# Four DMA turns of a feed-forward moved from SyncE's queue to ScalarE's

## The chip, the cores and the metric

The kernel runs on 1 core of one Trainium2 chip. The metric is the device time of one execution in microseconds; the kernel before has a median of 1064.58 us in 3 runs (1063.89 to 1068.48). TensorE, VectorE (DVE), ScalarE (ACT), GpSimd (POOL) and SyncE (SP) each work through a queue of their own and meet by semaphores.

## The reference

Two layers over x of 256 rows by 1024, all in float32. Each layer is: a half-step SwiGLU feed-forward, a token mixer, and a second half-step feed-forward. The change touches the feed-forwards alone:

```python
def _swiglu(h, w_gate, w_up, w_down):
    return (jax.nn.silu(h @ w_gate) * (h @ w_up)) @ w_down

x = x + 0.5 * _swiglu(_rms_norm(x, ffn1_norm[l]), ffn1_w_gate[l], ffn1_w_up[l], ffn1_w_down[l])
```

with D_MODEL 1024 and D_FF 2816. The mixer (a convolution of width 31, latent attention with 8 heads, gates and an output projection) stands between the two feed-forwards of a layer.

## The kernel before

**Products in three parts.** Every float32 product is made of three float32r products on TensorE: high by high, low by high and high by low (`products`, lines 602 to 606). So each weight unit of 128 x 2048 is loaded by SP into one of 3 raw buffers, rounded by ScalarE into `whi` (`split`, line 1044), and its rest is written by VectorE into `wlo` (`split`, line 1390). `whi` and `wlo` are rings of 6 units. SP may load a unit once VectorE has finished the rest of the unit three before it (`place`, line 360 issues).

**A feed-forward.** There are four, named (l, f) here: layer l, half f. D_FF is cut into NCH = 11 chunks of 256 columns. Chunk c has two units of gate and up weights and one of down weights, so the units of a feed-forward are: 0 and 1 for gate_up(0), then 2, 3 for gate_up(1), 4 for down(0), 5, 6 for gate_up(2), 7 for down(1), and so on; 32 is down(10), and in a first half 33 and 34 are the mixer's first two (w_in). TensorE does gate_up(c) for row tiles t = 0 and 1 (24 matmuls each), then down(c - 1) for both (12 each). Between gate_up(c) and down(c) the chunk's value has to be transposed:

- ScalarE `silu(c, t)` (line 1101) and VectorE `mul(c, t)` (line 1465) make the gated value of a row tile in `gu`.
- ScalarE `split_planes(c, t)` (line 1110) rearranges it as 16-bit words into `planes`, which lies in tile `qkT`; it counts up `planes_ready`.
- A DMA transposes `planes` into `turned`, also in `qkT`: this is the turn (`plane_turn`, line 385, `dma_start_transpose`). It waits for both planes and for `joined` of the turn before, so one turn is in flight at a time.
- VectorE `join(c)` (line 1478) puts the words together again in `vtok`, ScalarE `round_joined(c)` (line 1118) rounds to `gThi`, VectorE `rest_joined(c)` (line 1395) writes `gTlo`, and TensorE's down(c) waits for that.

The last chunk, c = 10, is transposed by TensorE instead (`turn`, line 716; `round_gu`, line 1126; `rest_gu`, line 1395); this `rest_gu` stands in VectorE's queue behind the split of unit 33 in a first half.

**Orders written out by hand.** SP's order in a feed-forward (lines 391 to 408) is gate_up(c) units, then the turn of chunk c - 2, then down(c - 1), for c from 1 to 10. The turn of chunk 9 (NCH - 2) stands outside: after a first half between the two halves of the first w_in block (line 431), after the second half of layer 0 in the next layer's first loads (line 400), and at the very end (line 451). ScalarE's order in chunk 0 is `first` (line 1129): split 2, silu(0,0), squares, split 3, planes(0,0), silu(0,1), split 4, planes(0,1). In chunks 1 to 9 it is `pair` (line 1140): round_joined of the chunk before, split, silu, split, planes, silu, split, planes. VectorE's has join(c - 1), rest_joined(c - 1), then split, mul, split, mul, split (lines 1487 ff.); in chunk 0 split 4 is its last item ahead of join(0). At the end ScalarE splits unit 32, then does round_joined(9), silu(10,0) and, in a first half, split 33.

Of the kernel before, what the change touches and what calls it, by code (L numbers as in the profile page):

```python
# [27 lines left out]
DEPTH = 2  # L28
# [86 lines left out]
def trunk(nc, a):  # L115
    with ExitStack() as ctx:
# [190 lines left out]
        def per_turn(l, f, c):  # L307
            return (l * 2 + f) * (NCH - 1) + c + 1
# [45 lines left out]
        @block.sync  # L354
        def _(sp):
            def place(l, u, u0, pairs):

                sp.wait_ge(wlo_ready, l * U_LAYER + u + 1)
                for dst, src in pairs:
                    sp.dma_start(dst, src).then_inc(raw_landed[slot(u0, RAW)], 16)  # L360

            def gate_up(l, f, c, c0, h):
                u0 = unit_gu(f, c0, h)
                dst = raw[:, slot(u0, RAW), 0:2048].rearrange("p (k g n) -> p k g n", k=4, g=2)
                rows = slice(4 * h * P, 4 * (h + 1) * P)
                cols = bass.ds(c * FC, FC)
                place(l, unit_gu(f, c, h), u0, [
                    (dst[:, :, g, :], w[l, rows, cols].rearrange("(k p) n -> p k n", p=P))
                    for g, w in enumerate((wg[f], wu[f]))])

            def down(l, f, c, c0):
                u0 = unit_down(f, c0)
                dst = raw[:, slot(u0, RAW), 0:2048].rearrange("p (k n) -> p k n", k=2)
                place(l, unit_down(f, c), u0, [
                    (dst[:, k, :], wd[f][l, bass.ds(c * FC + k * P, P), :]) for k in range(2)])

            def load_gain(l):

                sp.dma_start(gain[:, :], norms[1][bass.ds(l, 1), :].to_broadcast([P, D])).then_inc(gain_landed, 16)

            def plane_turn(l, f, c):

                sp.wait_ge(planes_ready, per_turn(l, f, c) * TT)
                sp.wait_ge(joined, per_turn(l, f, c))
                sp.dma_start_transpose(turned[:, :, :], planes.rearrange("p b k t f -> p (b k t f)")
                                       ).then_inc(turned_landed, 16)

            def ffn(l, f):
                def first():
                    if l == 0 and f == 0:  # L390
                        first_unit(sp, 0, 0)
                        second_tile(sp, 0)
                        first_unit(sp, 1, 0)
                        for t in range(TT):
                            sp.dma_start(posi[:, t:t + 1], a["positions"][0, t * P:(t + 1) * P].unsqueeze(1)
                                         ).then_inc(small_landed, 16)
                    else:
                        gate_up(l, f, 0, 0, 0)
                        if f == 0:
                            plane_turn(l - 1, 1, NCH - 2)  # L400
                        gate_up(l, f, 0, 0, 1)

                first()
                for c in range(1, NCH):
                    gate_up(l, f, c, c, 0)
                    gate_up(l, f, c, c, 1)
                    if c > 1:
                        plane_turn(l, f, c - 2)
                    down(l, f, c - 1, c - 1)
                down(l, f, NCH - 1, NCH - 1)  # L410

            def block_of(l, u, w, r0, k, c0, n):

                dst = raw[:, slot(u, RAW), 0:k * n].rearrange("p (k n) -> p k n", k=k)
                src = w[l, r0:r0 + k * P, c0:c0 + n].rearrange("(k p) n -> p k n", p=P)
                h = k // 2
                place(l, u, u, [(dst[:, h:k], src[:, h:k]), (dst[:, 0:h], src[:, 0:h])])

            sp.dma_start(x[:, 0, 0:512], a["x"][0, 0:P, 0:512]).then_inc(x_first, 16)

            for l in range(DEPTH):
                ffn(l, 0)
                load_gain(l)

                sp.wait_ge(vec_used, l + 1)
                sp.dma_start(vec[:, :], a["vec"][l]).then_inc(vec_landed, 16)
                for n, w in enumerate((a["q_norm"], a["k_norm"])):
                    sp.dma_start(qkg[:, n, :], w[bass.ds(l, 1), NOPE:QK].to_broadcast([P, ROPE])).then_inc(vec_landed, 16)
                for h in range(2):
                    if h == 1:  # L430
                        plane_turn(l, 0, NCH - 2)
                    block_of(l, UM + M_PR + h, a["w_in"], 4 * h * P, 4, O1, PR)
                def conv_units(base, j):
                    for g in range(2):
                        block_of(l, UM + base + g, a["w_in"], 0, KD, g * C + j * 256, 256)

                conv_units(M_C01, 0)
                block_of(l, UM + M_UQ, a["w_uq"], 0, 2, 0, H * QK)
                block_of(l, UM + M_UKV, a["w_ukv"], 0, 2, 0, H * (NOPE + VD))
                conv_units(M_C23, 1)  # L440
                for g in range(4):
                    for h in range(2):
                        block_of(l, UM + M_G + 2 * g + h, a["w_in"], 4 * h * P, 4, O4 + g * C, C)
                for h in range(2):
                    block_of(l, UM + M_MLA + h, a["w_mla_out"], 2 * h * P, 2, 0, D)
                for h in range(2):
                    block_of(l, UM + M_CO + h, a["w_conv_out"], 2 * h * P, 2, 0, D)
                for h in range(4):
                    block_of(l, UM + M_WO + h, a["w_out"], 2 * h * P, 2, 0, D)
                ffn(l, 1)  # L450
            plane_turn(DEPTH - 1, 1, NCH - 2)

            sp.wait_ge(x_new, 6 * DEPTH + 1)
            sp.dma_start(a["out"][0, 0:P, :], x[:, 0, :]).then_inc(stored, 16)
            for h in range(2):
                sp.wait_ge(last_new, h + 1)
                sp.dma_start(a["out"][0, P:SEQ, h * 512:(h + 1) * 512], x[:, 1, h * 512:(h + 1) * 512]).then_inc(stored, 16)
            sp.wait_ge(gain_landed, 16 * DEPTH)
            sp.wait_ge(stored, 16 * 3)
# [578 lines left out]
        def _(act):  # L1038
            def split(l, u0, turns=0):

                n = (l * (U_LAYER // RAW) + turns + (u0 // RAW + 1)) * 32
                act.wait_ge(raw_landed[slot(u0, RAW)], n)
                act.wait_ge(unit_free, l * U_LAYER + turns * RAW + (u0 + 1))
                nc.scalar.activation(whi[:, slot(u0, RING), 0:USED[u0]], raw[:, slot(u0, RAW), 0:USED[u0]],  # L1044
                                     ACT.Copy).then_inc(whi_ready, 1)
# [47 lines left out]
            def ffn(l, f):  # L1093
                def silu(c, t):
                    if t == 0:
                        act.wait_ge(gu_done, l * (2 * NCH) + c + (NCH * f + 1))
                    else:
                        unit_released(act, l, unit_gu(f, c, 1))
                    if isinstance(c, int) and c == 0:
                        act.wait_ge(rs_ready, per_norm(l, 2 * f, t))  # L1100
                    nc.scalar.activation(sgate[:, t, :], bank[:, 4 + t, 0:FC], ACT.Silu,  # L1101
                                         scale=rs[:, t:t + 1]).then_inc(silu_ready, 1)

                def split_planes(c, t):
# [4 lines left out]
                    words = gu[:, t, :].bitcast(U16).rearrange("p (k f b) -> p b k f", k=2, b=2)  # L1109
                    nc.scalar.activation(planes[:, :, :, t, :], words, ACT.Copy).then_inc(planes_ready, 1)  # L1110

                def round_joined(c, c0):

                    act.wait_ge(joined, per_turn(l, f, c) + 1)
                    if not (isinstance(c, int) and c == 0):

                        unit_released(act, l, c * 3 + (UB[f] - 2))
                    nc.scalar.activation(gThi[:, (c0 % 2) * 2:(c0 % 2) * 2 + 2, :], g_turned.rearrange("p (k n) -> p k n", k=2),  # L1118
                                         ACT.Copy).then_inc(ghi, 2)
# [10 lines left out]
                def first():  # L1130
                    split(l, UB[f] + 2)
                    silu(0, 0)
                    norm_squares(l, 2 * f, 1)
                    split(l, UB[f] + 3)
                    split_planes(0, 0)
                    silu(0, 1)
                    split(l, UB[f] + 4)
                    split_planes(0, 1)

                def pair(c, c0, i=0):  # L1140
                    u = UB[f] + 2 + 3 * c0
# [10 lines left out]
                with act.Fori(0, (NCH - 3) // 2) as i:  # L1152
                    pair(i * 2 + 1, 1, i * 2)
                    pair(i * 2 + 2, 2, i * 2)
                pair(NCH - 2, NCH - 2)
                c = NCH - 1
                if f == 0:
                    split(l, UB[f] + 2 + 3 * c)
# [686 lines left out]
```

## Time and profile before

| | |
|---|---|
| median of 3 runs | 1064.58 us (1063.89 to 1068.48) |
| profiled execution | 1062.78 us, span 1060.9 us |
| PE busy | 1048.6 us |
| DVE busy | 673.2 us |
| ACT busy | 560.1 us |
| POOL busy | 229.5 us |
| granted TensorE clock | 1.000 of full |
| bytes moved | 205.06 MB, 193 GB/s on average |
| DMA issues of w_down units, half a unit each | 88, 512.0 KB, median 5.4 us to landing |

A busy time is the sum over an engine's instructions; TensorE's matmuls overlap, so neighbours start closer together than each lasts. In the timelines a row begins with its start in us from the span's start and its duration; the bracket at its end is the idle time of the engine before it and what ended it. TensorE's first down product stands at 35.15 us in (0,0), 375.03 in (0,1), 556.87 in (1,0) and 899.09 in (1,1).

### The profile page before, as it was taken

What the parts mean: (1) busy time and instruction counts of PE and PEld (TensorE: products, weight loads), DVE (VectorE), ACT (ScalarE), POOL (GpSimd) and SP (SyncE); (2) the same over time, 40 slices, a digit from 0 to 9 for tenths busy, and PEclk for the clock granted to TensorE, in tenths of its full rate; (3) what the DMA queues carried; (4) which work ended last, traced back from release to release, by engine and by line L of the source; (5) the groups of instructions that cost most, each with busy time, mean ns of one, the idle gap of its engine ahead of it and who ended that gap; (6) DMA issues with size and microseconds to landing.
All of it is one profiled execution on the core that took longest, in us unless ns stands there. A gap on an engine that the chain in (4) does not pass through costs nothing. (4 is left out here: it accounts for less than half of the span.)

```text
span 1060.9 us, 13912 instructions
## 1 busy us (share of the span) xinstructions
PE 1048.6 (99%) x5100; PEld 878.8 (83%) x5100; DVE 673.2 (63%) x899; ACT 560.1 (53%) x732; POOL 229.5 (22%) x258
## 2 busy tenths in 40 slices
PE   8999999999999999999999999999999999999998
PEld 5888887998888888888888888879988887888887
DVE  6556556599976465565656546556999665564563
ACT  6445445575762554454455535536767535454461
POOL 1840000049850000000048000002589300000000
PEclk9999999999999999999999999999999999999999
DMA  8776786365645367767656686674366345867761
GB/s 277 220 230 202 211 242 225 127 219 169 208 149 179 95 203 218 225 200 219 217 159 204 186 249 204 206 247 157 132 209 232 105 159 129 220 203 220 225 203 48
DMA packets 176701, 205.06 MB, mean 193 GB/s; under 512 B 49264, under 2 KB 147856, under 8 KB 176656
## 3 DMA queue, kind: packets, MB, share of 16 engines
q1 hardware_dynamic: 174064, 200.78, 61.3%
q10 hardware_dynamic: 2592, 3.69, 1.2%
q8 instruction: 27, 0.44, 0.2%
q14 instruction: 18, 0.15, 0.0%
HBM read 192.90 MB, written 1.05 MB: 183 GB/s over the span
## 5 line engine op out<-in xcount | busy, mean ns | idle before, releaser
L1390 DVE TENSOR_TENSOR wlo<-raw,whi 128x2048 fp32r<-128x2048 f32 x154 | 351.4, 2286 | 69.1 <-ACT whi L1044 69.0
L604 PE MATMUL bank<-whi,hThi 128*128 128x512 f32 (+1 forms) x976 | 379.2, 388 | 0.3 <-DVE wlo L1390 0.3
L606 PE MATMUL bank<-whi,hTlo 128*128 128x512 f32 (+1 forms) x976 | 373.7, 383 | 0.0
L605 PE MATMUL bank<-wlo,hThi 128*128 128x512 f32 (+1 forms) x976 | 373.6, 383 | 0.0
L1044 ACT ACTIVATE whi<-raw 128x2048 fp32r<-128x2048 f32 x178 | 338.7, 1908 | 16.2 <-DMA raw<-in_ffn_w_up 7.9
L604 PEld LDWEIGHTS bank<-whi,hThi 128*128 128x128 f32 x976 | 183.4, 188 | 36.0 <-DVE wlo L1390 0.7
L606 PEld LDWEIGHTS bank<-whi,hTlo 128*128 128x128 f32 x976 | 183.2, 188 | 35.8
L605 PEld LDWEIGHTS bank<-wlo,hThi 128*128 128x128 f32 x976 | 183.5, 188 | 34.2
L1118 ACT ACTIVATE gThi<-vtok 128x512 fp32r<-128x512 f32 x40 | 25.3, 632 | 277.1 <-DVE vtok L1478 237.8
L604 PE MATMUL bank<-whi,gThi 128*128 128x512 f32 (+1 forms) x416 | 162.7, 391 | 2.7 <-DVE gTlo L1395 2.7
L605 PE MATMUL bank<-wlo,gThi 128*128 128x512 f32 (+1 forms) x416 | 161.2, 387 | 0.0
L606 PE MATMUL bank<-whi,gTlo 128*128 128x512 f32 (+1 forms) x416 | 161.2, 387 | 0.0
L472 POOL TENSOR_TENSOR small<-small,expo 128x1 f32<-128x1 f32 (+3 forms) x20 | 21.7, 1087 | 602.6 <-DVE small L1399 562.5
L1478 DVE COPY vtok<-qkT 128x1024 uint16<-128x1024 uint16 x40 | 30.2, 755 | 166.6 <-DMA qkT<-qkT 166.4
L586 POOL TENSOR_TENSOR wlo<-raw,whi 128x2048 fp32r<-128x2048 f32 x24 | 110.2, 4604 | 19.1 <-ACT whi L1044 18.8
L1557 DVE SCALAR_TENSOR_TENSOR bank<-cu,vec,bank 128x256 f32<-128x256 f32 x240 | 97.3, 484 | 0.1
L604 PEld LDWEIGHTS bank<-whi,gThi 128*128 128x128 f32 x416 | 78.1, 188 | 19.7 <-DVE gTlo L1395 4.3
L606 PEld LDWEIGHTS bank<-whi,gTlo 128*128 128x128 f32 x416 | 78.1, 188 | 16.1
L605 PEld LDWEIGHTS bank<-wlo,gThi 128*128 128x128 f32 x416 | 78.2, 188 | 15.3
L1110 ACT ACTIVATE qkT<-gates 128x512 uint16<-128x512 uint16 x80 | 50.0, 625 | 23.9 <-DVE gates L1465 23.9
L1101 ACT ACTIVATE gates<-bank,small 128x256 f32<-128x256 f32 x88 | 40.5, 460 | 19.1 <-PE bank L606 17.8
L1395 DVE TENSOR_TENSOR gTlo<-vtok,gThi 128x512 fp32r<-128x512 f32 x40 | 27.7, 692 | 35.5 <-ACT gThi L1118 35.5
(163 smaller groups left out, 805.8 us busy)
## 6 DMA issues: line engine op xcount, KB each, us to landing
raw<-in_ffn_w_down SPq DMA_DIRECT2D x88, 512.0 KB, 5.4
raw<-in_ffn_w_gate SPq DMA_DIRECT2D x86, 512.0 KB, 4.2
raw<-in_ffn_w_up SPq DMA_DIRECT2D x86, 512.0 KB, 5.3
raw<-in_w_in SPq DMA_DIRECT2D x48, 512.0 KB, 4.9
raw<-in_w_out SPq DMA_DIRECT2D x16, 512.0 KB, 4.4
raw<-in_w_in SPq DMA_DIRECT2D x8, 544.0 KB, 7.6
raw<-in_w_mla_out SPq DMA_DIRECT2D x8, 512.0 KB, 3.9
raw<-in_w_conv_out SPq DMA_DIRECT2D x8, 512.0 KB, 4.8
```

The source lines that it names most:

```text
L586: nc.gpsimd.tensor_tensor(wlo[:, slot(u, RING), 0:n], raw[:, slot(u, RAW), 0:n], whi[:, slot(u, RING), 0:n].bitcast(F32), ALU.subtract).th ...
L604: nc.tensor.matmul(out, lh, rh, start=start, stop=False, skip_group_check=skip)
L605: nc.tensor.matmul(out, lh, rl, start=False, stop=False, skip_group_check=skip)
L606: return nc.tensor.matmul(out, ll, rh, start=False, stop=stop, skip_group_check=skip)
L1044: nc.scalar.activation(whi[:, slot(u0, RING), 0:USED[u0]], raw[:, slot(u0, RAW), 0:USED[u0]], ACT.Copy).then_inc(whi_ready, 1)
L1101: nc.scalar.activation(sgate[:, t, :], bank[:, 4 + t, 0:FC], ACT.Silu, scale=rs[:, t:t + 1]).then_inc(silu_ready, 1)
L1110: nc.scalar.activation(planes[:, :, :, t, :], words, ACT.Copy).then_inc(planes_ready, 1)
L1118: nc.scalar.activation(gThi[:, (c0 % 2) * 2:(c0 % 2) * 2 + 2, :], g_turned.rearrange("p (k n) -> p k n", k=2), ACT.Copy).then_inc(ghi, 2)
L1390: nc.vector.tensor_tensor(wlo[:, slot(u0, RING), 0:n], raw[:, slot(u0, RAW), 0:n], whi[:, slot(u0, RING), 0:n].bitcast(F32), ALU.subtract) ...
L1395: return nc.vector.tensor_tensor(out, in_, hi.bitcast(F32), ALU.subtract)
L1478: nc.vector.tensor_copy(g_turned.bitcast(U16).rearrange("p (n b) -> p b n", b=2), turned.rearrange("p (b j) r -> p b (j r)", b=2)).then_in ...
L1557: ins = nc.vector.scalar_tensor_tensor(out=o, in0=i, scalar=w, in1=o, op0=ALU.mult, op1=ALU.add)
```

## The change

The turns of chunk 0 and of chunk 9 of every feed-forward are issued by ScalarE; those of chunks 1 to 8 stay with SP. ScalarE issues the turn of chunk 9 right behind planes(9,1), ahead of the split of unit 32. In chunk 0 planes(0,1) moves ahead of split 4, and the turn stands between the two. The waits of a turn are the same ones.

```diff
@@ SP
                     else:
                         gate_up(l, f, 0, 0, 0)
-                        if f == 0:
-                            plane_turn(l - 1, 1, NCH - 2)
                         gate_up(l, f, 0, 0, 1)
...
-                    if c > 1:
+                    if c > 2:
                         plane_turn(l, f, c - 2)
                     down(l, f, c - 1, c - 1)
...
                 for h in range(2):
-                    if h == 1:
-                        plane_turn(l, 0, NCH - 2)
                     block_of(l, UM + M_PR + h, a["w_in"], 4 * h * P, 4, O1, PR)
...
                 ffn(l, 1)
-            plane_turn(DEPTH - 1, 1, NCH - 2)
@@ ScalarE
+                def plane_turn(c):
+
+
+                    act.wait_ge(planes_ready, per_turn(l, f, c) * TT)
+                    act.wait_ge(joined, per_turn(l, f, c))
+                    act.dma_start_transpose(turned[:, :, :], planes.rearrange("p b k t f -> p (b k t f)")
+                                            ).then_inc(turned_landed, 16)
...
                     split_planes(0, 0)
                     silu(0, 1)
+                    split_planes(0, 1)
+                    plane_turn(0)
                     split(l, UB[f] + 4)
-                    split_planes(0, 1)
...
                 pair(NCH - 2, NCH - 2)
+                plane_turn(NCH - 2)
                 c = NCH - 1
```

## Rows read from the trace of the kernel before

**Rows 1.** DMA issues, whole span: count, KB each, median us to landing
```profile
raw<-in_w_in SPq DMA_DIRECT2D x8, 544.0 KB, 7.6
...
bias<-in_gate_bias ACTq DMA_DIRECT2D x8, 256.0 KB, 4.3
```

**Rows 2.** Waits of TensorE's weight loads: us in total, times, longest us
```profile
PEld bank L604 <- DVE gTlo L1395: 4.3, 4, 1.2
```

**Rows 3.** TensorE's timeline at its stalls: start us, us, what, [idle before <-releaser]
```profile
34.04 0.39 PE L605 MATMUL bank<-wlo,hThi 128*128 128x512 f32 x1
34.27 0.39 PE L606 MATMUL bank<-whi,hTlo 128*128 128x512 f32 x1
35.15 0.50 PE L604 MATMUL bank<-whi,gThi 128*128 128x512 f32 x1 [0.49 <-DVE gTlo L1395]
...
183.50 0.50 PE L604 MATMUL bank<-whi,gThi 128*128 128x512 f32 x1 [0.68 <-DVE gTlo L1395]
...
702.78 0.44 PE L716 MATMUL bank<-ident,gates 128*128 128x128 f32 x2 [1.59 <-DVE gates L1465]
...
706.65 0.50 PE L604 MATMUL bank<-whi,gThi 128*128 128x512 f32 x1 [0.68 <-DVE gTlo L1395]
...
899.09 0.50 PE L604 MATMUL bank<-whi,gThi 128*128 128x512 f32 x1 [0.80 <-DVE gTlo L1395]
```

**Rows 4.** ScalarE's timeline, (1,1), first chunk
```profile
887.45 0.47 ACT L1101 ACTIVATE gates<-bank,small 128x256 f32<-128x256 f32 x1 [0.92 <-PE bank L606]
887.82 1.91 ACT L1044 ACTIVATE whi<-raw 128x2048 fp32r<-128x2048 f32 x1
889.63 0.61 ACT L1110 ACTIVATE qkT<-gates 128x512 uint16<-128x512 uint16 x1
```

**Rows 5.** VectorE's timeline, (1,1), first chunk
```profile
888.26 0.48 DVE L1465 SCALAR_TENSOR_TENSOR gates<-bank,small,gates 128x256 f32<-128x256 f32 x1
889.76 2.29 DVE L1390 TENSOR_TENSOR wlo<-raw,whi 128x2048 fp32r<-128x2048 f32 x1 [1.02 <-ACT whi L1044]
896.69 0.75 DVE L1478 COPY vtok<-qkT 128x1024 uint16<-128x1024 uint16 x1 [4.63 <-DMA qkT<-qkT]
```

**Rows 6.** SP's timeline, (1,1), first chunk
```profile
890.27 1.25 SPq L385 DMA_TRANSPOSE qkT<-qkT  x1
892.08 0.86 SPq L360 DMA_DIRECT2D raw<-in_ffn_w_down  x2
```

**Rows 7.** VectorE's and SP's timelines, (0,0), first chunk
```profile
26.06 0.48 DVE L1465 SCALAR_TENSOR_TENSOR gates<-bank,small,gates 128x256 f32<-128x256 f32 x1
...
32.73 0.76 DVE L1478 COPY vtok<-qkT 128x1024 uint16<-128x1024 uint16 x1 [3.90 <-DMA qkT<-qkT]
...
27.23 1.92 SPq L385 DMA_TRANSPOSE qkT<-qkT  x1
```

**Rows 8.** ScalarE's, VectorE's and SP's timelines, (1,0), its end
```profile
689.99 0.61 ACT L1110 ACTIVATE qkT<-gates 128x512 uint16<-128x512 uint16 x1
...
701.80 2.01 ACT L1044 ACTIVATE whi<-raw 128x2176 fp32r<-128x2176 f32 x1
...
700.07 0.75 DVE L1478 COPY vtok<-qkT 128x1024 uint16<-128x1024 uint16 x1 [4.30 <-DMA qkT<-qkT]
...
706.18 0.42 DVE L1395 TENSOR_TENSOR gTlo<-bank,gThi 128x256 fp32r<-128x256 f32 x1
...
690.84 3.40 SPq L385 DMA_TRANSPOSE qkT<-qkT  x1
```

**Rows 9.** VectorE's and SP's timelines, (0,0), its end
```profile
176.91 0.75 DVE L1478 COPY vtok<-qkT 128x1024 uint16<-128x1024 uint16 x1 [3.94 <-DMA qkT<-qkT]
...
168.86 2.23 SPq L385 DMA_TRANSPOSE qkT<-qkT  x1
```

**Rows 10.** Tile qkT: all turns, ns min/median/max of the issue; us to landing
```profile
L385 SPq DMA_TRANSPOSE qkT<-qkT x40: 1232/2048/3403, 27.2 to 1032.9; - x40
...
DMA to landing us min/median/max: 3.0/6.2/9.2
```


## The prediction

> **What bounds the kernel now.** I read the page first, then the waits of TensorE, then the timelines of all queues around each place where TensorE waited. The page (the table above) has TensorE busy for 1048.6 us of 1060.9: only what lets TensorE wait costs time. Its 512-column matmuls start 0.23 us apart while each lasts 0.39 [rows 3], so a wait loses the idle time in the brackets plus 0.16 us, and the first matmul behind it lasts 0.50 instead of 0.39: another 0.11. Among the waits of the weight loads the largest with a releaser is gTlo L1395, the feed-forward's transposed operand: 4.3 us in 4 times [rows 2]. Naming a feed-forward (layer, half), the stalls that count are:
> - (0,0), first chunk's down product: 0.49 + 0.16 + 0.11 = 0.76 us.
> - (0,0), end: 0.68 + 0.27 = 0.95 us, at 183.50.
> - (1,0), end: 1.59 + 0.16 = 1.75 us before the transposes at 702.78, and 0.68 + 0.27 = 0.95 at 706.65.
> - (1,1), first chunk: 0.80 + 0.27 = 1.07 us, at 899.09.
> Together 5.5 us, 0.5% of the time [rows 3]. The middle two feed-forwards' first chunks do not stall, nor do the ends of (0,1) and (1,1). That 5.5 us is all the change can reach.
>
> **Why they stall.** First chunk of (1,1): ScalarE does silu(0,1) at 887.45, split 4 (887.82, 1.91 us), planes(0,1) at 889.63 (0.61 us) [rows 4]; SP issues the turn at 890.27 [rows 6]; VectorE joins at 896.69 [rows 5]: 6.42 us for a turn whose landing times over the kernel are 3.0/6.2/9.2 us [rows 10]. TensorE gets its operand 2.40 us behind the join's start (899.09 - 896.69) [rows 3, 5]. End of (1,0): turn issued at 690.84, join at 700.07, 9.23 us later [rows 8]. SP's order (lines 431 and 432) puts a w_in block's loads (median 7.6 us to landing [rows 1]) right ahead of it in the same queue. I read this as a turn that lands when what stands ahead of it in SP's queue has landed. The last turn, with nothing left to load beside it, lands in the 3.0 us of [rows 10].
>
> **First chunk, four times.** Moved ahead of split 4: planes(0,1) and the turn. Put behind them: split 4. Removed: nothing. Planes(0,1) now waits for mul(0,1) on VectorE, which split 4 used to cover: in (1,1) mul ends at 888.26 + 0.48 = 888.74 [rows 5], planes run 888.77 to 889.38, and the turn goes at 889.43, 0.84 us earlier than before. The turn holds ScalarE's queue. No row shows a turn issued from ScalarE; SP's take 1.23 to 3.40 us, median 2.05 [rows 10]. The long ones stand where loads fill SP's queue (3.40 at 690.84 [rows 8]); the one at 890.27 takes 1.25 and the next issue comes 1.81 behind it [rows 6]. ScalarE's queue is empty here, so I take D = 1.81 us, and keep 1.25 and 3.40 as ends. Split 4 then starts at 889.43 + D, takes 1.91, VectorE's half 2.29 [rows 4, 5], and that half stands ahead of the join in VectorE's order: the join can't start before 889.43 + D + 4.23 = 895.47. Its operand is there 2.40 later, 897.87; TensorE is ready at 898.13 (899.09 - 0.96). The stall of 1.07 goes if the turn lands by 895.73, that is within 6.3 us. Gain 1.07.
> The slack is thus 898.13 - 897.87 + 1.81 - D = 2.07 - D. The first chunks of (0,1) and (1,0) have the same order around them and TensorE at the same pace, so the same slack holds: 0.26 us are left at D = 1.81, and they stay without a stall.
> (0,0) differs. There mul(0,1) ran late, from 26.06 to 26.54, and the turn went at 27.23 [rows 7]. Planes can't run earlier, so the turn isn't issued any earlier, while split 4, which filled the wait for mul, is now pushed to 27.23 + D: join not before 27.23 + D + 4.23 = 33.27, where it was 32.73 [rows 7]. Here the edit costs 0.54 us (nothing at D = 1.25, 2.1 at 3.40).
> Sum of the first chunks: 1.07 - 0.54 = +0.5 us gained.
> SP, freed of the turn, still can't load down(1) at once: the raw buffer is released by split 4's VectorE half, in (1,1) now at 895.5 against 892.08 before [rows 6]. Its split comes behind the join (0.75), round_joined, two other splits (1.91 each), two silu and planes, over 6 us, and such a load lands in 5.4 us (the table's median): hidden, by about a microsecond at the least, and not late for TensorE, which wants it a chunk later.
>
> **Last but one chunk, four times.** The turn goes right behind planes(9,1) from ScalarE, ahead of one split. In (1,0): planes end at 689.99 + 0.61 = 690.60, turn at 690.65, nearly as before (690.84); the gain is the other queue. What landing on its own queue? Lower end 3.0 [rows 10], upper end the 9.2 of before; small loads from ScalarE's queue land in 4.3 us (median, 256 KB) [rows 1], the nearest row, also beside SP's loads; I take 4.5. The split behind the turn starts at 690.65 + D = 692.46, its VectorE half ends at 692.46 + 1.91 + 0.03 + 2.29 = 696.7, and the join follows there instead of at 700.07 [rows 8]. Then silu(10,0) waits for TensorE alone, and TensorE's wait of 1.75 goes. The second stall hangs on what follows: from the start of split 33 at 701.80 to the end of rest_gu at 706.18 + 0.42 pass 4.80 us [rows 8]. TensorE, with both waits gone (706.65 - 0.84 - 1.75), wants that at 704.06. Silu(10,0) can start once gate_up(10,0) is done, 12 matmuls of 0.23 before 701.03, at 698.3; split 33 (0.35 behind it, as silu and split follow each other in [rows 4]) at 698.65, if w_in is there: issued up to 1 us ahead of 690.84 with a median of 7.6, and the turn now shares the engines with it, so 697.5 to 700. That gives rest_gu at 703.5 to 704.8, a rest of 0 to 0.8; I count half of 0.95 as gone. Gain 1.75 + 0.5 = 2.2 us, between 0 (landing of 9.2) and 2.7.
> (0,0), end: turn at 168.86, join at 176.91 [rows 9]; with 4.5 us to land the join comes at about 175 (behind the delayed split), w_in (ahead of 168.86 by up to 1 us, median 7.6) has landed when silu(10,0) is through, and I take the 0.95 as gone, between 0 and 1.1. Gain 0.9.
> (0,1) and (1,1), ends: ScalarE stood idle for long before round_joined, so D is hidden; the join comes up to 1.7 us later and is still ahead of TensorE. 0, and -0.5 at the longest D.
> SP's w_in loads behind the old turn go up to 1.9 us sooner; hidden.
>
> **Sum.** 0.5 + 2.2 + 0.9 = 3.6 us off the profiled execution's 1062.78 us (span 1060.9). That execution lies 1.8 us under the median of 1064.58; I carry the difference over: 1064.58 - 3.6 = 1061.0 us. With both ends: best 1.07 + 0 + 2.7 + 1.1 = 4.9 gained, worst below.
>
> **A rule that speaks against it.** The rows show turns landing right behind what SP's queue holds [rows 8, 10], and 4.3 us for ScalarE's loads [rows 1]. The Trainium skill (DMA: Bandwidth & Descriptors, "Issuing engines are not separate DMA queues") says that transfers from several issuing engines end up on the same 16 DMA engines and interleave, so that another issuer saves only the issue time. The same page ("Queues, rings and completion order") has each DMA engine take turns between rings, packet by packet, which would let the short turn overtake. No row shows a turn beside a full other queue. By the first alone the gains at the ends vanish (sum 0.4 us), which is the first rival; by the second they come as forecast (3.6 us).
>
> **Rivals.**
> - First: no overtaking. The turn on ScalarE's queue lands as late as before, since the same engines move the same bytes: 9.2 us behind its issue in (1,0). Then both ends give 0. The first chunks give +0.9 in (1,1) (issued 0.84 earlier) and -0.54 in (0,0): 0.4 us, 1064.2. For it: the loads ahead of the turn keep the same engines busy. Against: ScalarE's 256 KB loads at 4.3 us [rows 1].
> - Second: slower. ScalarE is held as SP at its worst, D = 3.40. By the slack 2.07 - D each first chunk stalls 1.33 + 0.11: -2.1 in (0,0), -1.4 in (0,1) and (1,0) each, -0.4 in (1,1), sum -5.3; ends +2.1. Net 3.2 slower: 1067.8. It decides at D of about 2.8, where the gains at the ends are used up. For it: the SP median of 2.05 is near the slack. Against: SP's long ones have a full queue ahead, ScalarE's has none.
> - Third: all four stalls go, w_in lands in time and ScalarE is held for 1.25 us: 4.9 us, and more where the turns of unprofiled executions land later than in this profile (the runs reach 1068.48): 1059.0.
> - Fourth: no effect, as TensorE's lost time returns at the mixer, whose inputs could be late by themselves. Nothing in the slices of the page has TensorE below 9 tenths behind the start, so I see no such place. 1064.5.
>
> **How the numbers follow.** Forecast 0.50, first rival 0.16, second 0.08, third 0.21, fourth 0.05. What a measurement of this kernel can tell is about 0.5%, 5.3 us. The forecast, the first and the fourth lie within it; the third is at its edge, half of it beyond (0.10), with 0.04 from the forecast where turns of the timed runs landed later than the profile's; the second passes it only beyond D = 3.9: 0.03 with what I can't name. So faster 0.14, same 0.83, slower 0.03. The range, 1058.5 to 1065.5, holds the forecast, the first, the fourth and most of the third, and leaves out the far half of the second and what lies beyond the third.
>
> **What would show it.** DMA_TRANSPOSE on ACT's queue eight times, 1.2 to 1.8 us each (second rival: above 2.5); turns at the ends of (0,0) and (1,0) landing in 3.5 to 5.5 us (first rival: 8 to 9); no idle TensorE before the transposes at the end of (1,0); (1,1)'s first chunk without a stall; (0,0)'s first stall grown from 0.49 idle to about 1.0; SP's down(1) load 3 to 4 us later. If the first chunks of (0,1) and (1,0) stall, the slack was misread.

## The result, and the profile after

The changed kernel takes 1074.03 us in the median of 20 runs (1066.12 to 1077.84), the one before 1063.96 us in 20 runs beside it (1060.25 to 1068.48). The ratio is 1.009, with a 95% interval of 1.0074 to 1.0105: slower by 0.9%. (A ratio in this document is not exactly the quotient of the two medians.) I had forecast 1061.0 us and a range up to 1065.5.

The profiled execution (1067.3 us, span 1065.2) is among the quick ones of these 20; a second profile of the same kernel, below, shows a common one.

**What went as forecast.** Tile qkT of the changed kernel, the turns by issuing queue (ns min/median/max of the issue), then us to landing; answers to [rows 10]:

```profile
L385 SPq DMA_TRANSPOSE qkT<-qkT x32: 1238/1574/3047, 42.6 to 1020.8; - x32
...
L1111 ACTq DMA_TRANSPOSE qkT<-qkT x8: 1249/1273/3951, 27.2 to 1037.2; - x8
...
DMA to landing us min/median/max: 3.1/5.8/14.3
```

Eight turns come from ScalarE, with a median of 1.27 us for the issue, but one is issued in 3.95 us, and one lands after 14.3 us where the longest was 9.2. TensorE's timeline at the first down products of (0,0), (0,1) and (1,1); answers to [rows 3]:

```profile
35.49 0.50 PE L598 MATMUL bank<-whi,gThi 128*128 128x512 f32 x1 [0.86 <-DVE gTlo L1399]
...
374.13 0.39 PE L598 MATMUL bank<-whi,gThi 128*128 128x512 f32 x1
...
903.43 0.50 PE L598 MATMUL bank<-whi,gThi 128*128 128x512 f32 x1 [0.41 <-DVE gTlo L1399]
```

(0,0)'s wait grew from 0.49 to 0.86 idle, (1,1)'s fell from 0.80 to 0.41. The two nearly cancel. ScalarE's timeline in (1,1) shows how long the issue holds it:

```profile
894.16 1.27 ACTq L1111 DMA_TRANSPOSE qkT<-qkT  x1
895.54 1.92 ACT L1038 ACTIVATE whi<-raw 128x2048 fp32r<-128x2048 f32 x1 [1.41 <-issue]
```

Split 4 starts 1.38 us behind the issue, where I took D = 1.81.

The end of (0,0) has no stall in this profile, as forecast, but its turn took 6.5 us to land: more than the 3.5 to 5.5 that I had named as the sign.

**Where the time went.** TensorE's timeline at the end of (1,0); answers to 702.78 and 706.65 of [rows 3]:

```profile
699.93 0.39 PE L600 MATMUL bank<-whi,hTlo 128*128 128x512 f32 x1
706.57 0.69 PE L710 MATMUL bank<-ident,gates 128*128 128x128 f32 x2 [6.25 <-DVE gates L1469]
706.91 0.78 PE L598 MATMUL bank<-whi,gThi 128*128 128x512 f32 x1
...
708.76 0.63 PE L599 MATMUL bank<-wlo,gThi 128*128 128x512 f32 x1
...
710.85 0.39 PE L598 MATMUL bank<-whi,gThi 128*128 128x512 f32 x1
```

The wait before the transposes is 6.25 us idle instead of 1.59. Behind it, nine matmuls take from 706.91 to 710.85, 3.94 us instead of 9 x 0.23 = 2.07. That is the granted clock (PEclk, as a share of full speed), in TensorE's columns of the windows of the changed kernel (us, busy and count of each engine, then PEclk, DMA share, GB/s):

```profile
695.00:706.00 11.00, 5.32 (x24) 4.08 (x22) 3.61 (x3) 1.86 (x4) 0.00 (x0) 0.91 1.09 244
706.00:711.00 5.00, 4.43 (x12) 3.62 (x13) 3.89 (x5) 3.77 (x3) 0.00 (x0) 0.52 0.15 54
711.00:716.00 5.00, 5.00 (x24) 4.14 (x23) 2.93 (x2) 0.29 (x1) 0.00 (x0) 1.00 0.97 319
```

0.52 is the 1.2 GHz level for nearly all of that stretch. It had already fallen while TensorE stood idle (0.91 over the stretch that ends at 706), and was back at 2.4 GHz from 711. Before, behind its wait of 1.59 us idle, the same columns read:

```profile
700.00:706.00 6.00, 4.38 (x20) 3.00 (x18) 4.00 (x4) 5.08 (x5) 0.00 (x0) 1.00 0.93 326
```

Against 2.7 us lost there before, this end now loses 6.4 of wait (706.57 - 699.93 - 0.23) and about 1.9 of clock (3.94 - 2.07): 5.6 us more. The old second stall (0.95) is absent, as the slow matmuls give its input time. The end of (0,0) gained: the first down product of (0,0) starts 0.34 us later than before, that of (0,1) 0.90 us earlier (374.13 against 375.03), so 1.2 us were won between them. The two first chunks cancel, and the sum is 5.6 - 1.2 = 4.4 slower (the span says 4.3).

ScalarE's, VectorE's and SP's timelines at that end; answers to [rows 8]:

```profile
689.58 3.95 ACTq L1111 DMA_TRANSPOSE qkT<-qkT  x1
693.64 1.92 ACT L1038 ACTIVATE whi<-raw 128x2048 fp32r<-128x2048 f32 x1 [4.08 <-issue]
...
695.59 2.29 DVE L1394 TENSOR_TENSOR wlo<-raw,whi 128x2048 fp32r<-128x2048 f32 x1 [4.22 <-ACT whi L1038]
703.87 0.74 DVE L1482 COPY vtok<-qkT 128x1024 uint16<-128x1024 uint16 x1 [5.99 <-DMA qkT<-qkT]
...
688.23 0.45 SPq L426 DMA_DIRECT2D qkg<-in_k_norm  x1
688.72 10.16 SPq L360 DMA_DIRECT2D raw<-in_w_in  x6
```

The turn goes out 1.3 us earlier than before (689.58), 0.9 of it because TensorE itself is 0.9 us ahead here, and is joined 3.8 us later (703.87 against 700.07). SP, which used to issue the turn between the halves of w_in, now issues w_in straight through: the second half starts at 691.39, before at 694.29 behind the turn (SP's timelines, the changed kernel and the one before).

```profile
691.39 2.59 SPq L360 DMA_DIRECT2D raw<-in_w_in  x2
```

```profile
694.29 12.92 SPq L360 DMA_DIRECT2D raw<-in_w_in  x6
```

The DMA packets of 694 to 697 us, then 697 to 700 us, in the changed kernel (q1 is SP's queue, q10 ScalarE's; packets, MB, share):

```profile
q1 hardware_dynamic: 317, 0.60, 114.1%
q10 hardware_dynamic: 107, 0.03, 17.7%
...
q1 hardware_dynamic: 267, 0.54, 54.6%
q10 hardware_dynamic: 541, 0.14, 39.5%
```

Both queues share the engines from the turn's first packets on. Before, all of them stood in q1, the turn ahead of w_in's second half.

### The profile page after: what moved, and what is told of

Same layout as the page of the kernel before. It is cut to its first block and busy times, and to the rows that moved or that the text cites. A ratio compares the mean times of both kernels' runs of the same rounds, so it can differ in the third digit from the quotient of the medians.

```text
span 1065.2 us, 13912 instructions
## 1 busy us (share of the span) xinstructions
PE 1050.9 (99%) x5100; PEld 880.8 (83%) x5100; DVE 674.0 (63%) x899; ACT 562.3 (53%) x732; POOL 229.8 (22%) x258
```

## The experiments

Each names the kernel that it starts from; times are medians, with the kernel before beside them on the same chip, and ratios are to it. Where one time stands alone, the one before is that of the runs just above. A stall's "idle" is the time in its bracket.

**Which half of the change.** First chunk only (from before; SP's turns from c > 2, ScalarE's order as changed, turn of chunk 9 left with SP):

```diff
                     silu(0, 1)
+                    split_planes(0, 1)
+                    plane_turn(0)
                     split(l, UB[f] + 4)
-                    split_planes(0, 1)
```

> Chunk 0's half of the change alone: planes ahead of split 4 and the turn from ScalarE; the turns of chunk 9 stay with SP. Theory (the loss sits at the ends of the first halves, where the turn on ScalarE's own queue has to share the DMA engines with w_in loads that SP issues behind it): within 1.5 us of the kernel before, the wait before the first down product 0.8 to 1.2 us in (0,0) and under 0.7 in (1,1). Rival (ScalarE held by the issue, first chunks pay): 5 us or more slower.

Measured: 1061.71 against 1061.8 us, ratio 1.0006 (0.9992 to 1.002), with waits of 0.89 idle at (0,0)'s first chunk and 0.40 at (1,1)'s. This half is free. Last but one chunk only (from before; SP's turns of chunk 9 are taken out, which the cut leaves out):

```diff
                 pair(NCH - 2, NCH - 2)
+                plane_turn(NCH - 2)
```

> Chunk 9's half of the change alone. Theory: it holds the whole loss, 5 to 12 us slower than the kernel before, with a turn at the end of (1,0) that takes over 10 us to land and TensorE idle for over 4 us before its transposes. Rival (first chunks pay): within 1.5 us.

Measured: 1069.93 us, ratio 1.0089 (1.0069 to 1.011); the turn of (1,0) took 13.2 us to land, TensorE stood idle 5.2 us. The whole loss lies here (the full change has a ratio of 1.009). And only where no w_in follows (SP's turns of chunk 9 of the second halves are taken out):

```diff
                 pair(NCH - 2, NCH - 2)
+                if f == 1:
+                    plane_turn(NCH - 2)
```

> Only the turns of chunk 9 in the two second halves go to ScalarE, where SP has no w_in block behind them. Theory: within 1 us of the kernel before, those turns land in 3 to 6 us. Rival (a turn issued from ScalarE is slow or holds ScalarE wherever it stands): 2 us or more slower.

Measured: 1060.58 us, ratio 1.0006 (0.999 to 1.0021); both turns landed in 3.1 us. A turn issued from ScalarE is not slow by itself.

**Are the loads issued behind the turn to blame?** From the changed kernel, SP:

```diff
                 for h in range(2):
+                    if h == 1:
+                        sp.wait_ge(turned_landed, per_turn(l, 0, NCH - 2) * 16)
                     block_of(l, UM + M_PR + h, a["w_in"], 4 * h * P, 4, O1, PR)
```

> The changed kernel, but SP waits for the turn of chunk 9 to land before it loads the second half of the first w_in block, in (0,0) and (1,0). Theory (sharing with loads issued behind the turn): the turns land within 9 us, TensorE's wait before its transposes at the end of (1,0) falls from 6.2 us idle to under 2, the whole within 2 us of the kernel before. Rival (the turn is late because of the loads issued ahead of it, or because ScalarE's queue hands out its descriptors slowly): it still takes over 11 us, and the time stays near the changed kernel's, or above it as w_in comes later too.

Measured: 1062.46 us, ratio 1.0008 (0.9995 to 1.002). Issue and join of the turn in (1,0), 8.96 us apart:

```profile
692.42 1.65 ACTq L1113 DMA_TRANSPOSE qkT<-qkT  x1
...
701.38 0.76 DVE L1484 COPY vtok<-qkT 128x1024 uint16<-128x1024 uint16 x1 [2.96 <-DMA qkT<-qkT]
```

It lands after 8.9 us, within what SP's queue showed for this turn (6.6 to 9.2 us in four profiles with SP's turn and loads in the old order), and TensorE waits 0.94 idle instead of 6.25. So the loads issued behind the turn are needed for the loss. Is a second queue needed for the loss? From before, all turns from SP, the one of the first halves behind both halves of w_in:

```diff
                 for h in range(2):
-                    if h == 1:
-                        plane_turn(l, 0, NCH - 2)
                     block_of(l, UM + M_PR + h, a["w_in"], 4 * h * P, 4, O1, PR)
+                plane_turn(l, 0, NCH - 2)
```

> The kernel before, but SP issues the turn of chunk 9 in the first halves behind the second half of the first w_in block instead of between the halves. Theory (what slows the turn in the changed kernel is losing its place ahead of these loads, not that ScalarE issues it): it lands 10 to 14 us after its planes are ready in (1,0), TensorE waits over 3 us there, and the time is 4 to 12 us above the kernel before. Rival (a second queue is what hurts): lands 2 to 3 us later than before, under 3 us lost.

Measured: 1071.92 against 1062.94 us, ratio 1.0096 (1.0071 to 1.0122). TensorE before its transposes, at the ends of (0,0) and (1,0):

```profile
184.45 0.69 PE L715 MATMUL bank<-ident,gates 128*128 128x128 f32 x2 [4.42 <-DVE gates L1464]
...
710.43 0.44 PE L715 MATMUL bank<-ident,gates 128*128 128x128 f32 x2 [2.87 <-DVE gates L1464]
```

ScalarE's and VectorE's timelines there give the planes of (1,0) and its join, 10.9 us from the end of the one to the start of the other (before: 9.5):

```profile
696.17 0.62 ACT L1109 ACTIVATE qkT<-gates 128x512 uint16<-128x512 uint16 x1
...
707.73 0.74 DVE L1477 COPY vtok<-qkT 128x1024 uint16<-128x1024 uint16 x1 [6.80 <-DMA qkT<-qkT]
```

The loss is there without any turn from ScalarE (2.87 idle where I expected over 3 us), so giving up the place ahead of w_in's second half costs in one queue too. But it costs in another way. SP's timeline at the end of (1,0):

```profile
694.46 5.27 SPq L360 DMA_DIRECT2D raw<-in_w_in  x4
699.83 1.55 SPq L385 DMA_TRANSPOSE qkT<-qkT  x1
```

SP issues the four loads of w_in first, and the second two go out only at 698.63, once VectorE has freed their raw buffer (SP waits 3.2 us for it). So the turn goes out 3.0 us behind its planes, and then lands in 7.9 us, no later than before. Most of the loss is at the end of (0,0), where the turn was issued 3.2 us behind its planes and took 9.3 us. That a turn lands late beside the loads is shown by the held load, not by this kernel.

**The common run.** The changed kernel again:

> The changed kernel once more, unaltered, for a second profile and its time beside the next ones. If the loss is the turn of (1,0) alone: 1066 to 1069 us. If the more common times of 1074 to 1077 us have a cause of their own, the profile shows either a second long stall, at the end of (0,0), or a longer stretch at the lower TensorE clock.

Measured: 1071.98 us (1059.86 to 1075.68) against 1060.36, ratio 1.009 (1.0065 to 1.0114); the profiled execution took 1075.68 us. Its end of (0,0), ScalarE, VectorE and TensorE, then its windows:

```profile
171.27 2.16 ACTq L1111 DMA_TRANSPOSE qkT<-qkT  x1
...
183.77 0.74 DVE L1482 COPY vtok<-qkT 128x1024 uint16<-128x1024 uint16 x1 [5.99 <-DMA qkT<-qkT]
...
186.46 0.69 PE L710 MATMUL bank<-ident,gates 128*128 128x128 f32 x2 [4.45 <-DVE gates L1469]
```

```profile
180.00:186.00 6.00, 2.01 (x9) 1.31 (x7) 1.42 (x3) 1.41 (x3) 0.00 (x0) 0.97 1.04 278
186.00:192.00 6.00, 5.54 (x14) 4.47 (x15) 4.89 (x5) 3.67 (x3) 0.00 (x0) 0.50 0.24 69
```

So both answers hold: a second long stall at (0,0) (4.45 idle, where the first profile had none) and a second stretch at 1.2 GHz. I take it that whether (0,0) stalls, which differs between the two profiles, makes most of the spread from 1066 to 1078 us; two profiles don't prove it. One of these 10 runs took 1059.86 us with a granted clock of 1.000, so an execution without the loss exists too.

The traces show one thing that goes with it: how long behind SP's small loads the turn is issued. SP's and ScalarE's timelines at the end of (0,0), the first profile of the changed kernel:

```profile
164.69 0.47 SPq L426 DMA_DIRECT2D qkg<-in_k_norm  x1
...
169.25 1.69 ACTq L1111 DMA_TRANSPOSE qkT<-qkT  x1
```

and SP's in the second, whose turn stands above at 171.27:

```profile
167.82 0.43 SPq L426 DMA_DIRECT2D qkg<-in_k_norm  x1
```

4.6 us behind the load of k's gain the turn lands in 6.5 us, 3.5 us behind it in 12.5. In all traces here in which ScalarE issues the turn at these ends, with the load of k's gain ahead and w_in not held, seven turns issued 1.4 to 3.5 us behind that load landed in 11.4 to 14.9 us, and three issued 4.3 to 4.8 us behind it in 6.5 to 8.5. No run was made to test this.

**What the clock costs.** From the changed kernel, matmuls of zeros in the stall (bank 7's unread half):

```diff
                         gate_up(c, c, 1, halves=(0,))
+                        if f == 0:
+                            fill_wait(36 if l == 1 else 16)
                         turn(c, 0)
```

> The changed kernel with matmuls of zeros (into a part of a bank that nobody reads) just before the transposes of chunk 10 in the first halves: 36 of 256 columns in (1,0), some 3.9 us, and 16 in (0,0), some 1.7 us, so that TensorE works in the stall. Theory (part of the loss is TensorE's clock falling to half behind the stall): no matmuls 0.43 us apart behind it, 2 to 8 us faster than the changed kernel. Rival (only the wait counts): within 1 us of the changed kernel, or up to 2 us slower where the fill is longer than the stall.

Measured: 1070.45 us, 1.5 below the changed kernel measured beside it (4 and 10 runs, ranges overlap); ratio to before 1.0096 (1.0077 to 1.0116). The windows behind both stalls:

```profile
183.00:189.00 6.00, 3.78 (x20) 2.63 (x17) 4.08 (x6) 5.09 (x5) 0.00 (x0) 1.00 0.30 96
...
710.00:716.00 6.00, 4.84 (x25) 3.53 (x24) 4.82 (x5) 4.42 (x4) 0.00 (x0) 1.00 0.34 113
```

The clock stays at 1.00, but the time hardly moves: TensorE at full pace meets the next wait (the starts at 188.03 and 714.02 are followed by the next 1.07 and 1.06 us later, with 0.68 idle), which the slow matmuls had covered. This fits neither expectation exactly (2 to 8 us, or within 1 us), and with overlapping ranges the 1.5 us are not sure; most of the loss is the wait itself.

**What is under way ahead of the turn.** From before, the mixer's small loads (gain row, taps, q and k gains) behind the first w_in block:

```diff
-                load_gain(l)
-
-                sp.wait_ge(vec_used, l + 1)
-                sp.dma_start(vec[:, :], a["vec"][l]).then_inc(vec_landed, 16)
...
                     block_of(l, UM + M_PR + h, a["w_in"], 4 * h * P, 4, O1, PR)
+                load_gain(l)
+
+                sp.wait_ge(vec_used, l + 1)
+                sp.dma_start(vec[:, :], a["vec"][l]).then_inc(vec_landed, 16)
...
```

> The kernel before (all turns from SP), with the loads of the mixer's gain, taps and gains of q and k moved behind the two halves of the first w_in block, so that less stands ahead of chunk 9's turn in SP's queue. Theory (a turn lands when what SP issued ahead of it has landed): in (1,0) it lands within 7.5 us instead of 9.2, TensorE's wait of 1.6 us there goes, 1 to 3 us faster than before. Rival (landing is set by something else): no change.

Measured: 1059.18 against 1060.36 us, ratio 0.999 (0.998 to 1.0); at the bound of what can be told. Turn and join in (1,0) are 4.03 us apart instead of 9.23 (the turn lands in 3.5 us), and no stall is left at either end.

```profile
690.95 1.23 SPq L385 DMA_TRANSPOSE qkT<-qkT  x1
...
694.98 0.75 DVE L1478 COPY vtok<-qkT 128x1024 uint16<-128x1024 uint16 x1
```

The missing stalls alone prove little: the planes edit below, with the small loads still in front, has none either, and its turn of (1,0) landed in 6.6 us, issued 4.5 us behind the load of k's gain. But 3.5 us is less than in any of the profiles with them in front and the turn from SP (6.6 to 9.2).

The same edit on the changed kernel, with w_in's second half still issued behind the turn:

> The changed kernel with the small loads of the mixer moved behind the first w_in block, so that less of SP's work is under way when ScalarE issues the turn; w_in's second half is still issued behind it. Theory (sharing with the loads under way and behind it): the turn of (1,0) lands within 10 us instead of 13 to 14, and the time is 3 us or more under the changed kernel. Rival (only the loads issued behind the turn count): 12 to 14 us to land as in the changed kernel.

Measured: 1061.0 against 1062.94 us, ratio 0.9985 (0.9971 to 0.9998).

```profile
691.91 1.27 ACTq L1111 DMA_TRANSPOSE qkT<-qkT  x1
...
697.45 0.75 DVE L1482 COPY vtok<-qkT 128x1024 uint16<-128x1024 uint16 x1
```

It lands in 4.9 us beside w_in's loads (SP's next issue, the second half, is at 693.72). So loads issued behind the turn hurt only on top of what is under way ahead of it. The rival is out. That w_in's first half got a longer start is no explanation: it went out 2.4 us ahead of the turn here, and 2.6 and 2.7 us ahead of turns that took 13.6 and 13.2 us (second profile; chunk 9's half alone). Which of the small loads? From the changed kernel, only `load_gain(l)` moved:

> The changed kernel with only the mixer's gain load (512 KB) moved behind the first w_in block. Theory (it is bytes under way ahead of the turn that count; the gain has 512 of some 615 KB of the four small loads): the loss goes, within 2 us of the kernel before, the turn of (1,0) lands within 9 us. Rival (the many small packets of the taps and the q and k gains): still 5 us or more slower, landing in 12 us or more.

Measured: 1073.16 against 1060.14 us, ratio 1.0122 (1.0087 to 1.0157): the loss stays. In this profile it is the end of (0,0) that stalls (7.2 us idle, turn landing after 14.9 us), while (1,0)'s turn landed in 7.5. Only `vec` and `qkg` moved:

> The changed kernel with only the loads of taps and of q and k gains moved behind the first w_in block, the gain where it was. Theory (bytes): near the changed kernel, 5 us or more slower than before, landing in 11 us or more. Rival (small packets): within 2 us of the kernel before, landing within 9 us.

Measured: 1061.67 against 1060.14 us, ratio 1.002 (0.9998 to 1.0041), longest landing 9.0 us. My theory of bytes falls: the 71 KB of taps and 2 x 16 KB of q and k gains carry the loss. The gain's 512 KB are not free: with them alone in front the turn of (1,0) takes 9.0 us and TensorE waits 0.96 idle before its transposes, with none of the four loads in front 4.9 us and no wait; and two of the 10 runs took over 1066 us.

**Planes ahead of the split, without ScalarE's queue**, and then both edits that helped, from before:

```diff
                     silu(0, 1)
+                    split_planes(0, 1)
                     split(l, UB[f] + 4)
-                    split_planes(0, 1)
```

> The kernel before with one edit: planes(0,1) ahead of split 4 in ScalarE's order, the turn still from SP. Theory: the turn of (1,1) goes out 0.8 us earlier and split 4 is not held by the issue, so the first down product of (1,1) waits 0.3 us or less and the first of (0,0) no longer than before, 0 to 1 us faster in all, within the noise. Rival (ScalarE's waiting for mul costs as much as it gives): no change in either stall.

Measured: 1060.05 against 1060.36 us, ratio 0.9997 (0.9989 to 1.0006). The first down product of (0,0) no longer waits, that of (1,1) 0.2 us.

> All turns from SP, with both edits of the two kernels tried alone: planes(0,1) ahead of split 4, and the small loads of the mixer behind the first w_in block. Theory: their effects add, 1 to 3 us faster than the kernel before, no wait of TensorE over 0.5 us idle left at either end. Rival: the single gains were scatter, within 1 us of the kernel before.

Measured: 1059.81 against 1062.94 us, ratio 0.997 (0.9957 to 0.9984): the lowest ratio of all, and faster than both kernels. It is more than the two edits gave alone (1.2 and 0.3 us), so that they simply add is not shown.

## Why the prediction was wrong

**TensorE bounds it, four stalls of 5.5 us are all that can be won:** right as a ceiling for the gain. It said nothing of how large a stall can become.

**First chunks, +1.07 and -0.54:** right in direction, measured +0.39 and -0.37 idle. The hold D was 1.38 us instead of 1.81, but the (1,1) turn landed after 6.8 us where 6.3 were allowed, which left a stall. The middle two do not stall. The sum of this half is zero (ratio 1.0006).

**The end of (1,0): this is the step that failed.** I wrote "What landing on its own queue? Lower end 3.0 [rows 10], upper end the 9.2 of before; ... I take 4.5". It took 14.3 us, 13.6 in the second profile and 13.2 with this half alone. The upper end was no bound: it supposed that the turn keeps its place. In SP's queue it had w_in's second half behind it; on a queue of its own nothing keeps that half back. I had seen the move ("SP's w_in loads behind the old turn go up to 1.9 us sooner") and called it hidden, pricing what the earlier loads gain for themselves, not what they take from the turn; they went out 2.9 us sooner (691.39 against 694.29). The held load shows it: with the second half kept back until the turn has landed, the turn takes 8.9 us and the loss is gone. The forecast gain of 2.2 us at this end was a loss of 5.6. Beyond the landing, the fall of the clock behind a long wait stood in no term of the sum.

**The end of (0,0), +0.9:** came true in the first profile, by luck: the turn took 6.5 us where I had 4.5, and that was still soon enough. In the second it lost 4.45 us idle plus the clock. One profile of the kernel before could not tell that this place is on an edge: in the kernel with the first chunks alone changed, SP's own turn there landed after 9.4 us and TensorE waited 1.41 us idle.

**The rivals.** The first (no overtaking) was right about first chunks, and even too mild: the turns of (0,0), (0,1) and (1,0) land in 5.5, 5.9 and 5.8 us, from SP in 5.5, 4.4 and 5.0. The Trainium skill (DMA: Bandwidth & Descriptors, "Issuing engines are not separate DMA queues") has the transfers of all issuers interleave on the same 16 engines; the packet counts of both queues in one window agree. The Trainium skill's taking of turns, packet by packet (the same page, "Queues, rings and completion order"), from which I had hoped for an early landing, is no promise: at the end of (1,0) 107 packets of q10 (0.03 MB) moved beside 317 of q1 (0.60 MB) in 3 us, and 541 beside 267 in the next 3. The slower rival had the wrong mechanism: the issue did hold ScalarE for 3.95 us once, but where ScalarE had nothing urgent to do. The third (all four stalls gone) did not come: 0.86 and 0.41 us idle were left at the first chunks. The fourth (no effect) misses the measured ratio. No rival had the turn land later than before, or the clock fall.

**What stays open.** Why some 103 KB of small loads ahead of w_in make the turn so late. They alone do not (8.9 us with w_in held), nor do w_in's loads behind alone (4.9 us); only both, and only, in the traces here, where the turn is issued within 3.5 us of them. Nor is it separated whether SP's queue protects the turn by its order or by the time that its issue takes (before, the next load of w_in goes out 3.45 us behind the turn of (1,0), in the changed kernel 1.81). In the changed kernel w_in's first half, issued just ahead of the turn, also landed later, so it is not the turn alone that suffers. I did not separate taps from q and k gains.

## What to carry to other kernels

A DMA in the middle of a busy queue can be worth its place: at the end of (1,0) the turn landed in 9 us while w_in's second half waited behind it, and in 13 to 14 once it had left the queue. Before moving such a transfer to a queue of its own, ask what it was holding back, and bound its landing from above by all that can then be under way, not by its landing today. To bring a late transfer forward, first move what stands ahead of it and is not urgent; here that brought the landing from 9.2 to 3.5 us and needed no second queue.

## What the hardware showed unasked

- TensorE's clock fell to 1.2 GHz in a wait of 4.45 or 6.25 us idle, and stayed there for 4.3 us of matmuls behind the longer one (706.57 to 710.85) and for the 6 us from 186 behind the shorter; around the wait of 1.59 us of the kernel before it stayed at 1.00. Behind the 2.87 us idle of the kernel with the turn behind w_in it was still 1.00 when the matmuls resumed, and fell afterwards (0.50 from 712 to 714).
- A transpose issue takes 1.25 us at its quickest on ScalarE's queue (median 1.27) as on SP's (1.24, median 1.57), but up to 3.95 us where SP has many loads under way, although ScalarE's own queue is empty.
- At the end of (1,0) of the changed kernel the DMA engines moved next to nothing from 696 to 697.5 us, with four loads of w_in and the turn issued and not landed. The packets of that stretch, in the view used above:

```profile
q1 hardware_dynamic: 26, 0.05, 26.9%
q10 hardware_dynamic: 9, 0.00, 0.7%
```

No run here says why; it may be a part of what stays open.
